# Query projection cut into head units, modulation ahead of the transposes, sixteen early rows of the U table

## The reference

```python
hf = modulate(rmsnorm_2(x_lat, norm_ffn[l]), m_lat[3], m_lat[4])   # h * (1 + scale) + shift
q = (ht @ wq).reshape(n, 8, 2, 128)                 # 2048 x 2048 projection
s = einsum('nhpc,pkc->nhpk', q, keys)               # 128 scores per head and half
s1, i1 = top_k(s[:, :, 0], 16); s2, i2 = top_k(s[:, :, 1], 16)
sc, ci = top_k(s1[..., :, None] + s2[..., None, :], 16)   # 16 experts per head and token
e = i1[ci // 16] * 128 + i2[ci % 16]; gate = softmax(sc)
a = einsum('nd,nhkd->nhk', x, u_tab[e])             # 128 rows of U per token
out = einsum('nhk,nhkd->nd', gate * gelu(a), v_tab[e])    # 128 rows of V per token
```

## Time and profile before

| | us |
|---|---|
| median of three runs (2998.43, 3001.14, 3001.89) | 3001.14 |
| profiled execution, span | 3001.0 |
| first indirect DMA issued | 1693.8 |
| first one of the second choice issued | 1764.6 |
| last one issued | 2962.8 |
| busy PE / DVE / ACT / POOL | 2664.9 / 2058.4 / 1055.7 / 386.1 |

### The profile page before, as it was taken

The page is one execution under the profiler, slowest core; times in us unless marked ns, Lnnn a source line. Parts: engine busy times, 40 slices in busy tenths (PEclk is TensorE's granted clock), DMA queues, the critical chain, the costliest instruction groups (busy, mean ns, idle before and its releaser), DMA issues.

```text
span 3001.0 us, 28457 instructions
## 1 busy us (share of the span) xinstructions
PE 2664.9 (89%) x10052; PEld 1807.8 (60%) x10052; DVE 2058.4 (69%) x2510; ACT 1055.7 (35%) x1584; POOL 386.1 (13%) x401
## 2 busy tenths in 40 slices
PE   9999999999999999999999889877777777777773
PEld 7888888888888878888788754322222222222221
DVE  6675689999999987666566894676664554444446
ACT  5544443433333455635454422222222121111111
POOL 0000000000000000000000353211211121111112
PEclk9999999999999999999999999999999999999997
DMA  6454779888888964444354699999999999999997
GB/s 250 170 207 169 282 266 333 330 324 340 333 337 336 343 259 169 150 151 168 130 198 176 229 389 426 428 428 427 429 428 428 428 428 427 428 428 428 427 428 324
DMA packets 99086, 958.74 MB, mean 319 GB/s; under 512 B 11044, under 2 KB 11364, under 8 KB 13608
## 3 DMA queue, kind: packets, MB, share of 16 engines
q0 software_dynamic: 55552, 650.96, 52.2%
q1 hardware_dynamic: 43280, 305.91, 27.6%
q10 hardware_dynamic: 152, 0.53, 0.0%
HBM read 955.23 MB, written 2.13 MB: 319 GB/s over the span
## 4 chain that ended last, share of the span: by engine, by line
PE 59%; DMA 30%; DVE 7%; issue 2%; ACT 2%; POOL 0%; POOLq 0%; SPq 0%; DVEq 0%; ACTq 0%
DMA rows_g<-in_uv_tab_dram,idx 30%; PE bank L691 16%; PE bank L695 16%; PE bank L692 16%; PE bank L1259 6%; DVE rows_g L2737 4%; PE bank L725 1%; PE bank L1074 0%; PE bank L1019 0%; PE bank L733 0%; ACT diag L1829 0%; DMA ctx_x<-in_ctx_dram 0%; DVE split L1879 0%; POOL rows_g L665 0%; DMA raw<-in_wstream_dram 0%
## 5 line engine op out<-in xcount | busy, mean ns | idle before, releaser
L1259 PE MATMUL bank<-rows_g,diag 128*128 128x512 f32 x2000 | 918.7, 605 | 270.9 <-ACT diag L1829 270.9
L2737 DVE CUSTOM_DVE_ANT_0 rows_g<-rows_g,XN 128x2048 f32<-128x2048 f32 x256 | 596.7, 2333 | 542.1 <-DMA rows_g<-in_uv_tab_dram,idx 540.3
L1259 PEld LDWEIGHTS bank<-rows_g,diag 128*128 128x128 f32 x2000 | 365.0, 191 | 824.2 <-issue 824.0
L1879 DVE TENSOR_TENSOR split<-raw,split 128x2048 fp32r<-128x2048 f32 x282 | 645.3, 2289 | 283.6 <-ACT split L1273 277.7
L1273 ACT ACTIVATE split<-raw 128x2048 fp32r<-128x2048 f32 x286 | 547.8, 1917 | 674.3 <-DMA raw<-in_wstream_dram 661.9
L691 PE MATMUL bank<-split,UH 128*128 128x512 f32 x1936 | 764.5, 395 | 3.1 <-DVE split L1879 2.7
L695 PE MATMUL bank<-split,UL 128*128 128x512 f32 x1936 | 755.2, 390 | 0.0
L692 PE MATMUL bank<-split,UH 128*128 128x512 f32 x1936 | 754.6, 390 | 0.0
L665 POOL DMA_INDIRECT rows_g<-in_uv_tab_dram,idx x274 | 301.4, 1100 | 1080.9 <-PE bank L1259 858.5
L691 PEld LDWEIGHTS bank<-split,UH 128*128 128x128 f32 x1936 | 364.4, 188 | 79.1 <-issue 3.2
L695 PEld LDWEIGHTS bank<-split,UL 128*128 128x128 f32 x1936 | 364.1, 188 | 76.5
(11 more groups left out here) (417 smaller groups left out, 1442.2 us busy)
## 6 DMA issues: line engine op xcount, KB each, us to landing
raw<-in_wstream_dram SPq DMA_DIRECT2D x287, 1024.0 KB, 4.9
ada_w<-in_ada_dram POOLq DMA_DIRECT2D x96, 1024.0 KB, 7.1
rows_g<-in_uv_tab_dram,idx POOLq DMA_INDIRECT x274, 26.2
X<-in_x_dram SPq DMA_DIRECT2D x4, 512.0 KB, 9.4
c_row<-in_c_rows_dram POOLq DMA_DIRECT2D x1, 2048.0 KB, 8.5
ctx_x<-in_ctx_dram POOLq DMA_DIRECT2D x1, 2048.0 KB, 11.6
gb<-mod_rows POOLq DMA_DIRECT2D x2, 1024.0 KB, 5.9
raw<-in_wstream_dram SPq DMA_DIRECT2D x2, 512.0 KB, 6.7
```

Source lines behind the costliest of these rows:

```text
L1259: mm = pe.matmul(bank[4 * b + c], diag[:, n % DIAGS, :], v[:, c * CW:(c + 1) * CW], start=n in (0, SUMS_0), stop=n + 1 in (SUMS_0, len(SUMS)))
L1879: dve.tensor_tensor(WL[:, n % SLOTS_W, :], raw[:, n % SLOTS_W, :], WH[:, n % SLOTS_W, :].bitcast(F32), ALU.subtract).then_inc(lo_ready, 1)
L2737: dve.tensor_tensor_reduce(row(g), row(g), x, 1.0, 0.0, ALU.mult, ALU.add, dots[:, b, s:s + 1]).then_inc(sem("dot_done"), 1)
```

## The change

**Layout.** The first four chunks (tile 0) are laid out anew: the first 512 columns of the query matrix come as two units of 256 columns (head 0, head 1), each of two chunks with eight row blocks of 256 columns. `head_products` multiplies them with matmuls of 256 columns. Tiles 1 to 3 are as before. Head 0's scores are made inside head 1's unit.

**Modulation.** `modulated(r)` makes the modulated rows in token order first, in four parts of 512 columns; TensorE turns those, ScalarE and VectorE only copy and subtract. Lines 1333, 2659, 2661, 2728, 2730 go.

**Choice and order.** Head 0's choice stands right behind the low parts of chunks 2 and 3. Both `q_tok` copies are ScalarE's. `EARLY` is 16, so all slots of head 0 are single U rows and no pair can start before head 1's choice. `POOL_LO` is (4, 9, 11), ahead of gathers 0, 4 and 7. VectorE makes the low parts of 13 and 15.

```diff
-EARLY, LATE = 12, 6
+EARLY, LATE = 16, 6
-EARLY_DOTS = (0, 0, 0, 0, 0, 0, 1, 2, 1, 2, 1, 2, 1, 2, 0, 0)
+EARLY_DOTS = (0, 0, 0, 0, 1, 1, 2, 1, 2, 1, 2, 1, 2, 1, 1, 1)
-POOL_LO = (9, 11, 13, 15)
-POOL_LO_AT = (3, 6, 9, 12)
+POOL_LO = (4, 9, 11)
+POOL_LO_AT = (0, 4, 7)
+HEAD_W = 2 * NKEY
+HEAD_K = CK * CW // HEAD_W
...
+            def head_products(u, kk):
+                n, k = S_WQ + 2 * u + kk // HEAD_K, kk % HEAD_K
+                if k == 0:
+                    pe.wait_ge(lo_ready, n + 1)
+                if u == 0:
+                    pe.wait_ge(sem("u_ready"), KT * 4 + kk + 1)
...
+            for kk in range(KT):
+                if kk == CK or kk == 2 * CK:
+                    queries_turned(1 + kk // CK)
+                head_products(0, kk)
+            kept(1)
+            q_turned(0)
...
+            for kk in range(KT):
+                if kk == 2:
+                    scored((0, 1), 1, 0)
+                head_products(1, kk)
+            for t in range(1, OUT_TILES):
+                kept(t)
+                for m in range(CPT):
+                    if m == 1:
+                        kept(t + 1)
+                        for j in (1,) if t == 1 else range(2):
+                            q_turned(j)
+                    if m == 2:
+                        scored((2, 3) if t == 1 else range(2 * GH), 2 * t, 2 * t)
+                    products(S_WQ + CPT * t + m, ACC[(Q_WQ + t + 1) % 2], m * CK, CK, None, 0, UH, UL, first=m == 0, last=m == CPT - 1)
...
+            def to_q(u, c, width):
+                for b in range(NB):
+                    ins = act.activation(q_tok[:, b, c:c + width], ACC[(Q_WQ + u) % 2][b][:, 0:width], ACT.Copy)
+                ins.then_inc(acc_free_act, 1)
...
-            def scaled(r):
+            def modulated(r):
                 w = slice(r * CW, (r + 1) * CW)
                 for b in range(NB):
-                    ins = dve.tensor_scalar(XN2[:, b, w], X[:, b, w], rinv[:, b:b + 1], None, ALU.mult)
+                    link.mark(dve.scalar_tensor_tensor(XN2[:, b, w], X[:, b, w], rinv[:, b:b + 1], sc_row[:, w], ALU.mult, ALU.mult))
+                link.sync()
+                for b in range(NB):
+                    ins = dve.tensor_tensor(XN2[:, b, w], XN2[:, b, w], sh_row[:, w], ALU.add)
...
+            modulated(0)
+            modulated(1)
             queries_part(0)
+            modulated(2)
             queries_part(1)
+            modulated(3)
...
+            queries_part(2)
+            queries_part(3)
+            lo(S_WQ + 2)
+            lo(S_WQ + 3)
...
+            for _ in choose(0, 0, 0, 1):
+                pass
+            for m in range(3, OUT_TILES * CPT):
                 if m + LEAD not in POOL_LO:
                     lo(S_WQ + m + LEAD)
...
-                if m % CPT == CPT - 1:
-                    dve.wait_ge(split_used, S_WQ + m + 1)
-                    to_q((Q_WQ + m // CPT) % 2, m // CPT)
```

More of the change, by code:

```diff
@@ L1216, in stay_warm @@
                     pe.matmul(DB[3][:, 0:NB * P], ident_b[:, :], mask_b[:, :, :].rearrange("p d t -> p (d t)"), start=True, stop=True)
[L1218 to L1236, removed]
@@ new lines, in kept, with q_turned, scored @@
+            def kept(units):
+                pe.wait_ge(acc_free_act, Q_WQ + units + 2)
+            def q_turned(j):
+                for m in range(4):
+                    c = (2 * j + m // 2) * P
+                    mm = pe.transpose(DB[j][:, m * P:(m + 1) * P], q_tok[:, m % 2, c:c + P], ident[:, :])
+                mm.then_inc(sem("pq_turned"), 1)
+            def scored(lists, turned, kept_before):
+                pe.wait_ge(sem("q_t_ready"), turned)
+                if kept_before:
+                    pe.wait_ge(sem("key_s_ready"), kept_before)
+                for b in range(NB):
+                    for hp in lists:
+                        mm = pe.matmul(DB[2 + b][:, hp * NKEY:(hp + 1) * NKEY], q_t[:, hp, span(b)],
+                                       keys[:, hp % 2, :], start=True, stop=True)
+                    mm.then_inc(sem("key_ps"), 1)
@@ L1797, in exps @@
                 act.activation(gate_w[:, b, mine], gate_w[:, b, mine], ACT.Exp).then_inc(sem("exp_done"), 1)
[L1799 to L1817, removed]
-                        act.activation(key_s[b][:, 2 * GH * t:2 * GH * (t + 1), :],
-                                       DB[2 + b][:, :].rearrange("p (b t) -> p b t", t=NKEY), ACT.Copy).then_inc(
-                            sem("key_s_ready"), 1)
@@ L1824, in diagonal @@
+            exps(0, 0)
+            q_turned((2 * OUT_TILES - 2, 2 * OUT_TILES - 1))
+            act.wait_ge(sem("dot_done"), EARLY)
+            seq(act.activation(gelu_v[:, 0, 0:EARLY], dots[:, 0, 0:EARLY], ACT.Gelu_apprx_tanh))
+            scores(OUT_TILES, 2 * GH * (OUT_TILES - 1), 2 * GH)
             def diagonal(n, b, s):
@@ L2649, in scaled @@
                 ins.then_inc(sem("xn_ready"), 1)
[L2651 to L2652 removed]
             SIDE = ACC[(Q_WQ + 1) % 2]
             def queries_part(r):
[L2656 to L2663 removed]
+                banks = SIDE if r == 1 else DB[2 * (r % 2):2 * (r % 2) + 2]
@@ L2754, in later_choices @@
                     yield
-            later, rows = later_choices(), modulated()
-            for m in range(OUT_TILES * CPT):
+            later = later_choices()
+            for _ in choose(0, 0, 0, 1):
+                pass
+            for m in range(3, OUT_TILES * CPT):
                 if m + LEAD not in POOL_LO:
                     lo(S_WQ + m + LEAD)
-                if m < 2:
-                    queries_part(m + 2)
-                elif m < 6:
-                    next(rows)
-                if m == 5 or m == 14:
-                    for _ in choose(0, 0, 0 if m == 5 else 1, 1):
+                if m == 14:
+                    for _ in choose(0, 0, 1, 1):
                         pass
```

125 lines of the change are left out of this document (78 added, 47 removed).

## The result

The changed kernel takes **3008.41 us** (median of seven runs, 3004.73 to 3010.20) against 3000.40 of the kernel before beside it (seven runs, 2998.43 to 3001.89): a ratio of 1.0025, 95% interval 1.0016 to 1.0035. It is 8.0 us slower. The forecast was 3002.7, with 3008 as the upper end of the likeliest case; the time lies just above that, in the case "slower" (chance 0.27), and inside the range for eight in ten, 2990 to 3014.

The account below looks back on a forecast made before the run. DMA was taken as the bound, the end moving with its idle time before it stays full: -4.0 (earlier second choice) + 3.7 (fewer bytes) + 2.0 (empty queue) = +1.7 us on 3001.0, forecast 3002.7; eight in ten 2990 to 3014.

Parts of the forecast that it names:

- the likeliest case: Whole kernel: forecast within 0.2%, 3002.7 us, own range 2996 to 3008, second choice between 1753 and 1765; chance 0.45.
- the case "slower": Whole kernel: slower than forecast, chance 0.27, of which longer rounds of the three homes 0.20 and 256-column matmuls 0.07.
- First gather: Start of the modulation to head 0's choice: first gather issued at 1680.7, 13.1 us earlier than 1693.83.
- the rival with 0.19: Head units: 256-column matmuls cost 0.19 us each instead of 0.114, first gather 7 us later, 3014 us; chance 0.07.
- The lock: Head 0's choice: GpSimd's low part of chunk 4 shuts out VectorE's `cand`, 4.0 us taken out of 0 to 4.6.
- From there to the second choice: First gather to the second choice's first gather: 79.9 us instead of 70.74, so it goes out at 1760.6, 4.0 earlier.
- Gather 4 behind chunk 9's low part: GpSimd's queue: low part waits for ScalarE and a load, so the row lands some 2 us late: +2.0.
- DMA account: DMA up to where it stays full: -4.0 for the earlier second choice, +3.7 for bytes, +2.0 for latency, sum +1.7 us.
- Fewer bytes: DMA by the second choice: 30.2 MB moved instead of 31.8, 1.6 MB less: +3.7 us.
- Empty queue: DMA at the second choice: nothing queued, so the first gather's latency shows, +2.0 us out of 0 to 4.6.
- The signs: Wrong if share after second choice is under 1.00, that choice outside 1753 to 1765, or first gather under 10 us earlier.
- longer rounds: First gather to second choice: dots freeing the three homes queue behind low parts; 16.5 us a round gives 3010.7; chance 0.20.

Follow-up runs that it names:

- the run without the lock: Chunk 4's low part made by VectorE behind head 0's choice instead of by GpSimd, against the changed kernel: 3008.52 us, ratio 1.0028 to the kernel before.

## Why the prediction was right and wrong

The account (bytes and idle time of DMA up to the point from which it is full) and its mechanisms were right, the time was 5.7 us too low. By its own steps, counted from `rinv` (1642.03 before):

- **First gather.** Forecast 1680.7, which is +38.7; measured +40.6, so 1.9 late. That the clock times agree (1680.69) is chance, since this execution began 1.95 us earlier. Two terms. The first product starts at +7.3 instead of +6.3: the second part of the modulation is there 0.3 later than reckoned (+5.65), and the transposes ahead of the product take 1.6 us instead of 0.9. And the first twelve matmuls of 256 columns start 0.21 us apart before they fall to 0.12. The step took 0.114 from the earlier trace rows for all 96:

```profile
1649.64 0.41 PE L1232 MATMUL bank<-split,UH 128*128 128x256 f32 x1
1649.85 0.41 PE L1233 MATMUL bank<-split,UL 128*128 128x256 f32 x1
1650.06 0.32 PE L1231 MATMUL bank<-split,UH 128*128 128x256 f32 x1
...
1650.45 0.28 PE L1231 MATMUL bank<-split,UH 128*128 128x256 f32 x1
1650.57 0.28 PE L1232 MATMUL bank<-split,UH 128*128 128x256 f32 x1
```

  The granted clock is 0.66 on average from 1646 to 1652 and 1.00 after it, so the first matmuls ran at the lower of the two levels, 1.2 GHz. PE had been busy 2.26 of the 6 us ahead of 1646, where the kernel before was busy 4.56 and had 1.00. The eight transposes ahead of them took 1.97 us, where eight took 1.04 before. Twelve times 0.09 is 1.1 us. With 84 of the 96 matmuls at 0.12 us the rival with 0.19 is refuted.
- **The lock.** Forecast 4.0 on `cand`; it fell on the cast ahead of it, which takes 0.18 alone and took 4.10. The size was right, since the two stand next to each other and GpSimd's end decides; the instruction was wrong: the prediction looked only for two inputs in SBUF, and this one has one. The Trainium skill, page "SBUF — State Buffer", section "Who interferes with whom", also names `copy` and `cast` among the operations that can take the pair of ports shared with GpSimd, where their operands meet its conditions, and says that the other engine then "fully blocks"; the trace agrees with 4.10 against 0.18. More important: what the lock costs *the time* was put at 4 us, at unchanged work behind it; the run without it shows no difference (3008.52 beside 3008.41).
- **From there to the second choice.** Forecast 79.9, measured 82.30. The waits for rows were kept at 13.4 + 2.0 = 15.4 and came to 18.1. Gather 4 behind chunk 9's low part was priced at 2.0; it was issued 12.6 us after gather 3, and two of VectorE's waits for rows (2.76 and 6.42) follow. The price took the chunks as coming at their old pace; chunk 9 came 11.7 us later.
- **DMA account.** Second choice at +122.9 instead of +118.5: -4.0 became +0.4. Fewer bytes by then: 31.0 MB before and 29.5 after (253 GB/s in 122.54 us and 240 in 122.91), 3.5 us; forecast 3.7. Empty queue: 391 GB/s instead of 428 over 37.09 us is 3.2 us; forecast 2.0. Sum 0.4 + 3.5 + 3.2 = 7.1, measured 7.3.
- **The signs.** The prediction's own signs of being wrong include a share under 1.00 after the second choice. It is 0.94 over the first 37.09 us and 1.01 only after them, because the first row after the empty queue has to land: nothing moves from 1763 to 1765. The other two hold: the second choice at 1762.99 is inside 1753 to 1765, near its end, and the first gather is 11.2 us earlier.
- **The rivals.** The time came out near that of longer rounds (3010.7), but not mainly by them: only 2.4 us of the stretch can be theirs, and by that rival's reckoning a round came to (82.3 - 11) / 4.67 = 15.3 us, under the 15.7 from which it would decide. The run with 12 early rows took 13.6 us off and left the early part of the list as it is.

The step that was off, in one sentence: seven tenths of the earlier first choice were to be given back and all of it was (1.9 us more through the late first gather, 2.4 in the stretch behind it), and even an earlier first gather wouldn't have helped, as the run without the lock shows, because gathers 4 to 6 and 7 stand in a queue behind low parts whose chunks come when the weight stream brings them, and the new layout brings chunk 9 later. The prediction saw this wait and charged 2 us. The empty queue, at 3.2 instead of 2.0, adds 1.2. With 4.6 for two dots, 3.7 for the bytes and 2.0 for the queue it priced the four extra rows at 10.3 us, and so, for its sum of +1.7, everything else in the change at a gain of 8.6. The rows cost 13.6 (12.3 by the ratios), and everything else, with 12 early rows, was worth 4.6 (4.8). Both were off to the same side; no error hid the other.

## What to carry to other kernels

Ask of each earlier start what stands behind it in the same queue and waits for something else; where a queue mixes gathers with computation on data from another stream, the computation sets the pace. Ask too whether the change moves that other stream: here it put chunk 9 later by 11.7 us while the gathers came 11 us earlier. Work given to GpSimd to relieve VectorE is not free for VectorE: here 2.3 us saved stretched another instruction by up to 4 us and held gathers back by 5 to 15. Taking it all back was worth 6 us in the kernel before and in the kernel with 12 early rows and three such parts, and 16 in the one with four. Where one bound resource must be kept full, a single number (bytes moved up to the point from which it stays full) ordered all variants here, and a wait of the queue's feeder must have enough work queued ahead to outlast it.

## What was unexpected of the hardware

- A cast of 128x32 elements on VectorE took 4.10 us beside GpSimd's subtraction over 128x2048 that had begun 0.57 us before, against 0.18 without it. The FIND_INDEX8 of the same choice that began 0.25 us after GpSimd's start took 0.28, as elsewhere.
- A change of how a program fills its last 150 us before the steady part moved the end 1300 us later by 2.40 us for each MB not yet moved, to within 0.7 us, in 14 kernels.
